# GLA stage of an encoder trunk on one Trainium2 core: query scaling moved to GpSimd, second key buffer moved, four output blocks accumulated together, and x loaded ahead of weight blocks 1 and 2

## The reference, cut to what matters

```
q, k, v, g, lr = split(h @ w_in)
gk = log_sigmoid(lr @ w_gk2 + b_gk) / 16          # one set per direction
q = q * GLA_HK ** -0.5
per direction, per chunk of 64 tokens:
    gcum = cumsum(gk)
    q_t = q * exp(gcum);  k_t = k * exp(-gcum)
    att = where(causal, q_t @ k_t^T, 0)
    o = att @ v + q_t @ state;  state = state * exp(g_end) + (k * exp(g_end - gcum))^T @ v
o = rmsnorm(forward + backward, norm_w) * silu(g)
return o @ w_out
```

## Time and profile before

| | us |
|---|---|
| Median of 3 runs (1442.85 to 1446.71) | 1443.49 |
| The profiled execution, its own time | 1441.75 |
| Its span, first to last instruction | 1439.6 |
| PE busy in the span | 1379.3 (96%) |
| DVE / ACT / POOL busy | 822.8 / 646.5 / 639.9 |

### The profile page before, as it was taken

How to read it: one execution, slowest core, us unless ns; L and a number is a source line. 1 busy time by engine, 2 the same in 40 slices (tenths; PEclk the granted TensorE clock), 3 DMA queues, 4 the chain that set the end, 5 groups by cost and what they waited for, 6 DMA issues and landing times.

```text
span 1439.6 us, 16672 instructions
## 1 busy us (share of the span) xinstructions
PE 1379.3 (96%) x6690; PEld 1138.9 (79%) x6690; DVE 822.8 (57%) x981; ACT 646.5 (45%) x985; POOL 639.9 (44%) x291
## 2 busy tenths in 40 slices
PE   6999988989999999999999999987999999999997
PEld 6778656767888888888888877875798888888886
DVE  5657597662027998887001654355168998884003
ACT  4544685554245544344323475434454544343221
POOL 2345495024533554545544243422714645445550
PEclk9999999999999999999999999998999999999998
DMA  5222100112322323323332312201213232323331
GB/s 188 86 92 88 37 1 19 33 45 88 99 77 90 101 93 98 95 95 94 93 95 86 114 59 88 88 30 44 73 45 131 89 102 89 102 85 94 96 92 59
DMA packets 36766, 117.89 MB, mean 82 GB/s; under 512 B 3857, under 2 KB 8337, under 8 KB 36689
## 3 DMA queue, kind: packets, MB, share of 16 engines
q1 hardware_dynamic: 35888, 114.63, 25.1%
q10 hardware_dynamic: 800, 2.20, 0.5%
HBM read 114.58 MB, written 2.10 MB: 81 GB/s over the span
## 4 chain that ended last, share of the span: by engine, by line
PE 76%; DVE 6%; ACT 3%; POOL 2%; issue 1%; DVEq 0%; ACTq 0%; POOLq 0%
PE bank L315 23%; PE bank L316 23%; PE bank L317 23%; PE bank L1169 1%; PE bank L1301 1%; POOL ebuf L987 1%; PE bank L1302 1%; POOL xdt L973 1%; PE bank L1777 1%; PE bank L1324 1%; DVE xres L562 1%; PE bank L405 1%; ACT prob L1373 1%; DVE m_ffn L555 0%; PE bank L1505 0%
## 5 line engine op out<-in xcount | busy, mean ns | idle before, releaser
L298 POOL TENSOR_TENSOR wlo<-raw,whi 128x1024 fp32r<-128x1024 f32 (+2 forms) x216 | 530.7, 2471 | 697.3 <-ACT whi L292 697.3
L315 PE MATMUL bank<-xw_hi,whi 128*128 128x512 f32 (+1 forms) x1360 | 516.6, 380 | 16.3 <-DVE xw_lo L581 11.7
L317 PE MATMUL bank<-xw_hi,wlo 128*128 128x512 f32 (+1 forms) x1360 | 505.8, 372 | 0.0
L316 PE MATMUL bank<-xw_lo,whi 128*128 128x512 f32 (+1 forms) x1360 | 505.8, 372 | 0.0
L292 ACT ACTIVATE whi<-raw 128x1024 fp32r<-128x1024 f32 (+2 forms) x217 | 220.6, 1023 | 216.5 <-DMA raw<-in_fout 111.8
L315 PEld LDWEIGHTS bank<-xw_hi,whi 128*128 128x128 f32 x1360 | 259.9, 191 | 67.8 <-issue 16.4
L316 PEld LDWEIGHTS bank<-xw_lo,whi 128*128 128x128 f32 x1360 | 259.8, 191 | 47.3 <-issue 3.6
L317 PEld LDWEIGHTS bank<-xw_hi,wlo 128*128 128x128 f32 x1360 | 259.5, 191 | 45.1
L534 DVE RECIPROCAL small<-small 128x2 f32<-128x2 f32 (+1 forms) x12 | 2.0, 170 | 352.7 <-ACT small L471 337.4
L638 DVE SCALAR_TENSOR_TENSOR cbuf<-ubuf,par,cbuf 128x510 f32<-128x510 f32 x100 | 170.8, 1708 | 3.5
L315 PE MATMUL bank<-g_hi,whi 128*128 128x512 f32 (+1 forms) x396 | 146.0, 369 | 0.1
(11 more groups left out here) (251 smaller groups left out, 1435.2 us busy)
## 6 DMA issues: line engine op xcount, KB each, us to landing
raw<-in_fin SPq DMA_DIRECT2D x88, 512.0 KB, 3.5
raw<-in_fout SPq DMA_DIRECT2D x32, 448.0 KB, 3.2
raw<-in_gin SPq DMA_DIRECT2D x25, 512.0 KB, 3.6
raw<-in_hin SPq DMA_DIRECT2D x24, 512.0 KB, 3.6
raw<-in_hout SPq DMA_DIRECT2D x16, 512.0 KB, 3.5
raw<-in_fout SPq DMA_DIRECT2D x16, 512.0 KB, 3.5
raw<-in_gout SPq DMA_DIRECT2D x8, 512.0 KB, 3.6
xres<-in_x SPq DMA_DIRECT2D x8, 256.0 KB, 7.5
```

What stands on the lines that cost most here:

```text
L298: engine.tensor_tensor(wlo[s][:, 0:n], raw[s][:, 0:n], whi[s][:, 0:n].bitcast(F32), ALU.subtract).then_inc(w_lo, 1)
L315: first = nc.tensor.matmul(out_ap, wh, ah, start=start, stop=False)
L316: nc.tensor.matmul(out_ap, wh, al, start=False, stop=False)
L317: return first, nc.tensor.matmul(out_ap, wl, ah, start=False, stop=stop)
```

## The change

1. **Queries on POOL.** DVE's two query operations leave `dve_keys`. A new `pool_queries` does them as plain products on POOL; the factor `QG` moves into the mask constants and into the scale of `cross_scores`.
2. **Second keys.** `kk1` now lies over the four `cbuf` buffers, which the stage's squares leave for new tiles `gsq`. So keys of n = 0 and 1 are both formed during the input projection, and queries 0 and 1 too, on POOL between two weight splits.
3. **Order.** Square roots (`deviation`) move behind the last exponentials on ACT and a one-column exponential stands at the head of ACT's stage; `spread(0)` to `spread(3)` move to the last head and beyond; `sums(2)` and `sums(3)` stay near their places. DVE does the gating after all keys, and takes over the low parts of chunks 2 to 7.
4. **Four output blocks together.** Output blocks 0 to 3 are accumulated in banks 0 to 3 head by head (`outs` in `pe_gla`): two chunks of the operand into four banks, as soon as that head is gated, with sums(3) and the last two spreads between. The high and low parts of weight blocks `gout` + 3, + 4, + 5 are made inside the stage; the following four stand before chunk 4 in `act_out` and `pool_out`.
5. **Start.** SP issues weight block 0, then the four x transfers of request 0, weight block 1, the four of request 1, weight block 2; ACT issues the parameters' DMA. ACT splits weight block 1 after all of request 0 and block 2 after all of request 1. PE takes block 0 for both requests piece by piece (48 matmuls of 256 columns), then blocks 1 and 2 with 24 matmuls of 512 columns each.

```diff
-            kk1 = sb("kk1", NREQ * NCH * SEQ, F32, s)      # over the operand's region
+            kk1 = sb("kk1", NREQ * NCH * SEQ, F32, s)      # over cbuf
+            gsq = [sb(f"gsq{i}", T, F32, s) for i in range(4)]
@@ pe_start
-                for j in range(GROUP[-1]):
-                    product(pe, j, of_request(banks[j], r), xw_hi, xw_lo, r=r, wait=r == 0, last_of_block=r == 1,
-                            by_chunk=("res_lo", r * KD) if j == 0 else None)
+                product(pe, 0, of_request(banks[0], r), xw_hi, xw_lo, r=r, wait=r == 0, last_of_block=r == 1,
+                        by_chunk=("res_lo", r * KD))
+            for j in (1, 2):
+                product(pe, j, banks[j][:], xw_hi, xw_lo)
@@ sync
-            sp.dma_start(par[:], params).then_inc(sem("par_in"), 16)
-                    if r == 0 and i % 2:
-                        load(sp, 1 + i // 2)
                     sp.dma_start(ckr(xres, 2 * i, r, 2), x_in[...])
+                load(sp, 1 + r)
@@ dve_gin, pool_gin
                     dve_keys(dve, 0)
+                    dve_zero_keys(dve, 1)
+                    dve_keys(dve, 1)
+                if at == BASE["gin"] + 21:
+                    pool_queries(pool, 0)
+                    pool_queries(pool, 1)
+        def pool_queries(pool, n):
...
+            pool.wait_ge(sem("gla_e"), 2 * n + 1)
+            nc.gpsimd.tensor_tensor(qt[d][:], ck(gqkv, hd), qt[d][:], ALU.mult).then_inc(sem("gla_q"), 1)
+            pool.wait_ge(sem("gla_q"), 2 * n + 1)
+            if hd:
+                pool.wait_ge(sem("gla_s"), n - 1)
+            nc.gpsimd.tensor_tensor(qx[d][...], qt[d][...][:, :, c0:c0 + 2],
+                                    carries_of(hd, d)[:, :, 6:8].unsqueeze(3).broadcast_to([P, NREQ, 2, CH]),
+                                    ALU.mult).then_inc(sem("gla_q"), 1)
@@ pe_gla
+            def outs(hd):
+                for c in range(GROUPED[2]):
+                    if hd == 0:
+                        pe.wait_ge(w_lo, base + c + 1)
+                    for k in (2 * hd, 2 * hd + 1):
+                        if c == 0:
+                            pe.wait_ge(sem("gla_lo"), k + 1)
+                        first, last = three(base + c, bank[c][:], ck(xw_hi, k), ck(xw_lo, k), k, k == 0, k == KD - 1)
+                    if hd == GLA_HEADS - 1:
+                        last.then_inc(mm, 1)
                 if hd < 3:
                     scores(2 * hd + 2)
+                if hd == 3:
+                    spread(0)
                 values(hd)
+                if hd == 3:
+                    spread(1)
                 if hd:
                     sums(hd - 1)
                 if hd < 3:
                     scores(2 * hd + 3)
-                if hd:
-                    spread(hd - 1)
-            sums(GLA_HEADS - 1)
-            spread(GLA_HEADS - 1)
+            outs(0)
+            sums(3)
+            spread(2)
+            outs(1)
+            spread(3)
+            outs(2)
+            outs(3)
@@ act_gla
+            nc.scalar.activation(small[:, 5:6], prm("eps"), ACT.Exp)
             act_gate_exps(act, 2)
             cross_scores(0, 0)
+            for hd in range(3):
+                act_gate_exps(act, 2 * hd + 3)
                 cross_scores(hd, 1)
+                if hd < 2:
+                    act_gate_exps(act, 2 * hd + 4)
                     cross_scores(hd + 1, 0)
+                    outs(hd)
+            cross_scores(3, 0)
+            deviation(0)
+            outs(2)
+            deviation(1)
+            cross_scores(3, 1)
+            act.wait_ge(sem("gla_s"), 8)
+            high(0)
+            hi(act, BASE["gout"] + 3)
+            outs(3)
+            deviation(2)
             high(1)
             deviation(3)
@@ dve_gla
+            for n in range(2, 8):
+                dve_keys(dve, n)
+                own_scores((n - 1) // 2, (n - 1) % 2)
+            diagonal(0)
+            own_scores(3, 1)
+            gated(0)
+            diagonal(1)
+            gated(1)
+            diagonal(2)
+            low(1)
+            gated(2)
             diagonal(3)
+            low(2)
             gated(3)
+            low(3)
@@ pool_gla
+            for n in range(2, 8):
+                pool_queries(pool, n)
+                if n in (4, 6):
+                    squares(n // 2 - 2)
+            squares(2)
...
+            lo(pool, nc.gpsimd, BASE["gout"] + 3)
             squares(3)
```

More of the change, by code:

```diff
@@ L127, in build_program @@
             prob1 = sb("prob1", 4 * SEQ, F32, s)
+        with ExitStack() as s:
+            kk1 = sb("kk1", NREQ * NCH * SEQ, F32, s)
         cbuf = [sb(f"cbuf{i}", T) for i in range(4)]
@@ L348, in x_norm, with obank @@
             return ((k + 1) // 2) * 32 + ((k + 1) % 2) * 16
-        def obank(c):
-            return bank[c % 2]
+        def obank(k, c):
+            return bank[c if c < GROUPED.get(k, 0) else c % 2]
         def late_bank(k, c, r):
@@ L365, in pe_out @@
             base = BASE[name]
-            for c in range(EARLY[k]):
-                if c >= 2:
+            for c in range(GROUPED.get(k, 0), EARLY[k]):
+                if k in GROUPED:
+                    pe.wait_ge(sem("out_m"), of("out_m", k) + c - GROUPED[k] + 1)
+                elif c >= 2:
                     pe.wait_ge(sem("out_m"), of("out_m", k) + c - 1)
@@ L375, in pe_out @@
                             pe.wait_ge(sem(stage), n)
-                    product(pe, base + c * per + b, obank(c)[:], src_hi, src_lo, k0=k0,
+                    product(pe, base + c * per + b, obank(k, c)[:], src_hi, src_lo, k0=k0,
                             start=b == 0, stop=b == per - 1, by_chunk=first_by_chunk if c == 0 and b == 0 else None)
@@ L447, in act_out @@
             for c in range(EARLY[k]):
-                for b in range(per):
-                    his(act, base + c * per + b)
+                if c >= GROUPED.get(k, 0):
+                    for at in range(base + (1 if k in GROUPED and c == GROUPED[k] else c * per), base + (c + 1) * per):
+                        his(act, at)
                 act.wait_ge(mm, base + (c + 1) * per)
@@ L452, in act_out @@
                     act.wait_ge(sem("out_acc"), of("out_acc", k) + c - 2)
[L453 removed]
+                nc.scalar.activation(sqacc[:] if c == 0 else cbuf[c % 2][:], obank(k, c)[:],
                                      ACT.Square).then_inc(sem("out_sq"), 1)
[L455 removed]
+                nc.scalar.activation(ck(m_tile, c), obank(k, c)[:], ACT.Copy,
                                      scale=prm("norm", m_norm(k) + c)).then_inc(sem("out_m"), 1)
@@ L521, in pool_out @@
             for c in range(EARLY[k]):
-                for b in range(per):
-                    los(pool, base + c * per + b)
+                if c >= GROUPED.get(k, 0):
+                    for at in range(base + (1 if k in GROUPED and c == GROUPED[k] else c * per), base + (c + 1) * per):
+                        los(pool, at)
                 if c:
@@ L1715, in dve_keys @@
                 nc.vector.tensor_tensor(to, k[:, :, c], e[:, :, c], ALU.mult).then_inc(sem("gla_kk"), 1)
-            nc.vector.scalar_tensor_tensor(out=qt[d][:], in0=ck(gqkv, hd), scalar=QG, in1=qt[d][:],
-                                           op0=ALU.mult, op1=ALU.mult).then_inc(sem("gla_q"), 1)
             dve.wait_ge(sem("gla_kk"), 5 * n + 2)
-            carries = carry[:].rearrange("p (m r j) -> p m r j", r=NREQ, j=8)[:, d * GLA_HEADS + hd]
+            carries = carries_of(hd, d)
             for c in range(NCH):
@@ L1823, in cross_scores @@
                                          sbank(d, r)[:, d * SEQ + (1 - d) * P:d * SEQ + (2 - d) * P],
-                                         ACT.Copy).then_inc(sem("gla_att_b" if d else "gla_att_f"), 1)
+                                         ACT.Copy, scale=QG).then_inc(sem("gla_att_b" if d else "gla_att_f"), 1)
             def outs(hd):
@@ L1915, in diagonal, with low @@
                                             sem("gla_diag"), 1)
-            dve_keys(dve, 1)
-            own_scores(0, 0)
-            dve_keys(dve, 2)
-            for hd in range(GLA_HEADS):
-                own_scores(hd, 1)
-                if hd < 3:
-                    dve_keys(dve, 2 * hd + 3)
-                if hd >= 2:
-                    gated(hd - 2)
-                if hd < 3:
-                    own_scores(hd + 1, 0)
-                    if hd < 2:
-                        dve_keys(dve, 2 * hd + 4)
-                if hd:
-                    diagonal(hd - 1)
+            def low(hd):
+                if hd == 1:
+                    dve.wait_ge(sem("gla_lo"), 2)
+                dve.wait_ge(sem("gla_o"), 2 * hd + 2)
+                for c in (2 * hd, 2 * hd + 1):
+                    dve.wait_ge(sem("gla_hi"), c + 1)
+                    nc.vector.tensor_tensor(ck(xw_lo, c), ck(gg, c), ck(xw_hi, c).bitcast(F32),
+                                            ALU.subtract).then_inc(sem("gla_lo"), 1)
+            own_scores(0, 0)
```

(17 more changed lines are left out.)

58 lines of the change are left out of this document (20 added, 38 removed).

## The result

The changed kernel takes **1432.69 us** in the median of five runs (1427.66 to 1433.35), the kernel before 1443.19 (five runs, 1442.76 to 1446.71): a ratio of 0.991 on record, 95% interval 0.989 to 0.993 (the two medians alone give 0.993). The five runs fall into two groups, 1427.66 and 1428.8, and 1432.69 to 1433.35. The profiled execution took 1432.82 us, with a span of 1431.0.

The account below looks back on a forecast made before the run. The prediction took PE, busy for 96% of the span, as the bound. Gains of 6.5 (start) and 17.0 (GLA stage), 23.5 us, took the profiled 1441.75 to 1418.3; with 1.7 for the median, rounded, 1420, range 1412 to 1430.

Parts of the forecast that it names:

- The step that failed: GLA stage, DVE products beside POOL: 0.7 us more per us of overlap, so keys 2 take 2.2 us.
- rival B: POOL holds DVE for a whole POOL instruction; GLA keys come later, 10 us less gain, 1430; chance 0.10.
- was to give 17.0: GLA stage: output block 3 ends at 1015.8 us, 17.0 before 1032.8.
- the clock's term of 1.5: GLA stage: 1.5 us allowed for PE time at the half clock, with 0 and 4 as ends.
- The wait at the third scores: GLA stage: PE waits for keys 2 from 952.2 us, so scores(2) starts at 954.1.
- the offload yields next to nothing: GLA keys: removed query work about 0.95 us of DVE, added contention about 0.8.
- was to give 6.5: Start: blocks 0 to 2 end at 27.5 instead of 34.4 us; 6.5 taken, bounds 3.3 and 8.0.
- The forecast's ends for DVE, 15.4 and 17.5: Start: DVE's last low part of x at 15.4 us, or 17.5 if one piece again takes 2.58 beside POOL's split.
- A: Start gives half: clock low to 22.4 us or x not earlier, 3.3 instead of 6.5, 1423; chance 0.13.
- C: The clock falls twice more or POOL's adds come late: 4 us less gain, 1424; chance 0.12.
- E: The gain doesn't arrive: a later stage waits for something that did not move, as a DMA; 1435; chance 0.05.
- D: Slower than before: POOL's query pairs become the GLA stage's chain, 1445 us and over; chance 0.03.

Follow-up runs that it names:

- queries_dve: The changed kernel with the queries of pairs 2 to 7 back on DVE, POOL keeping 0 and 1: 1423.6 us.
- queries_behind: The changed kernel with POOL's product of a later query waiting until DVE's five products of the same pair's keys are done: 1426.16 us.
- ungrouped: The changed kernel without the four output blocks opened together; all six run one after another from the end of the last spread: 1438.33 us.
- both_dve: The changed kernel with the queries of the six later pairs and the low parts of weight blocks 1 and 2 back on DVE: 1422.08 us.
- start_only: The kernel before with the change of the start alone: 1439.33 us, ratio 0.9978.
- pool_quarters: The changed kernel with POOL's low parts of weight blocks 1 and 2 made in four instructions of 256 columns each: 1424.05 us.
- scores0_early: both_dve with the first scores and the third pair's exponentials and keys moved ahead into the GLA input projection's last block: 1419.57 us.

## Why the prediction was wrong

**The step that failed: "So I give each product of DVE with two SBUF operands 0.7 us more for each us of overlap with POOL".** The contention isn't a share but a hold, rival B's mechanism. In these traces a DVE instruction with two tensor operands in SBUF that starts while a POOL instruction on SBUF operands runs ends only 0.1 to 0.6 us behind POOL's. So what it loses is the rest of POOL's instruction: a low part takes 2.39 and 2.59 us instead of 0.47 at the start, and the key products 1.83 and 2.19 against a forecast of 2.2 for all of them. I read the gating product's 1.40 against 0.69 as a rate; it started 0.4 us behind a POOL instruction of 1.27 us and was held by the rest of that. Nor does the 2.2 follow from the rate: 0.7 for each of 1.7 us of overlap, on 1.58 alone, is 2.8. In the changed kernel the same product takes 2.48 and 2.02 beside whole splits of POOL, while the scaling product before it (L1926), with one operand in PSUM, takes its usual 0.75 in the middle of such a split:

```profile
1005.71 2.39 POOL L302 TENSOR_TENSOR wlo<-raw,whi 128x1024 fp32r<-128x1024 f32 x1 [4.50 <-ACT whi L296]
1006.17 2.48 DVE L1930 TENSOR_TENSOR gg<-gg,ubuf 128x512 f32<-128x512 f32 x1
...
1011.72 2.60 POOL L302 TENSOR_TENSOR wlo<-raw,whi 128x1024 fp32r<-128x1024 f32 x1 [3.62 <-ACT whi L296]
1012.06 0.75 DVE L1926 SCALAR_TENSOR_TENSOR ubuf<-gqkv,par,bank 128x512 f32<-128x512 f32 x1
1012.85 2.02 DVE L1930 TENSOR_TENSOR gg<-gg,ubuf 128x512 f32<-128x512 f32 x1
```

The Trainium skill (SBUF — State Buffer, Who interferes with whom) calls the pair of ports that both engines share an exclusive lock. It says that a VectorE instruction with two SBUF inputs contends for it with a GpSimd instruction that reads SBUF, and that one with at most one SBUF input, outside the 2-port modes, does not. The traces agree: 2.48 and 2.02 for the first kind, 0.75 for the second. The prediction rested on the Trainium skill's GPSIMD Engine Reference (Key points), which names the contention without its form.

**The GLA stage** was to give 17.0 and gave 10.4 (112.3 to 101.9), and 14.7 once the queries no longer meet DVE's products (97.6). So the hold cost 4.3 us. PE's waits account for them: 3.6 + 4.1 + 0.2 = 7.9 us in the changed kernel, 2.1 + 0.9 + 0.5 = 3.5 in queries_dve. The clock does not: its mean from 943 to 1040 us is 0.95 in both. Rival B's price of 10 us was too high: PE has 8.7 us of work for each head's two pairs, and only the first pair's keys and the adds were exposed. The remaining 2.3 us I put to the clock's term of 1.5, with bounds of 0 and 4, which no run separates: at queries_dve's 10.2 us of half clock up to 5.1 us of PE's work is lost. Right were POOL's pair (1.27 to 1.38 and 0.62 to 0.88) and the end of the diagonals' waits (0.2 left). The wait at the third scores was to be 1.9 and is 2.1 in queries_dve, but there DVE makes the queries itself, so the match is luck; with the queries on POOL and no hold on the keys it is 3.4 (queries_behind). That the offload yields next to nothing was too kind: beside the keys it costs the 4.3. The four output blocks carry the stage's gain, as forecast: ungrouped is 9.7 us longer.

**The start** was to give 6.5 and gave 2.9. The forecast's ends for DVE, 15.4 and 17.5, allow for one part held by POOL; two were (2.39 and 2.59), as in the kernel before (2.36 and 2.58, of which the earlier trace rows show only the longer), and DVE ended at 18.5. From this PE's gap of 1.89 followed, and behind it 3.4 us at the half clock, for which the sum had no term. With the splits elsewhere the sums come at 28.02, as in the forecast (28), and the gain is 7.1. So the walk held but for the hold: the same cause as in the stage, on a row that I had in the earlier trace rows and priced only as a bound.

**What reached the end.** 2.9 + 10.4 = 13.3; the spans differ by 8.6. The stretch between sums and values is 3.6 us longer (907.3 to 910.9), and the rest 1.0. Of the 15 us between the forecast gain and that of the profiled execution, the stage has 6.6 (4.3 of them the hold), the start 3.6 (the hold), and these two 4.6, for which the sum had no term: the prediction assumed that whatever is gained in one place arrives. In the eleven profiles the stretch took 905.9 to 911.0. Two places in it can be named. One is a fall of the clock near 50 us. All eleven have the same wait of 2.9 us there, for a weight block's low part that POOL makes; behind it the changed kernel goes on at 1.2 GHz and queries_dve at 2.4. Below are the first matmul behind the wait in these two, and then the same stretch of before, of the changed kernel and of queries_dve:

```profile
47.32 0.76 PE L319 MATMUL bank<-xw_hi,whi 128*128 128x512 f32 x1 [2.94 <-POOL wlo L302]
```

```profile
47.54 0.47 PE L319 MATMUL bank<-xw_hi,whi 128*128 128x512 f32 x1 [2.94 <-POOL wlo L302]
```

```profile
40.00:60.00 20.00, 17.06 (x69) 13.55 (x68) 15.16 (x18) 11.55 (x16) 5.25 (x3) 0.91 0.25 75
```

```profile
40.00:60.00 20.00, 17.06 (x63) 13.51 (x62) 14.67 (x16) 11.24 (x15) 6.59 (x3) 0.83 0.24 77
```

```profile
40.00:60.00 20.00, 16.39 (x72) 12.99 (x71) 16.72 (x18) 12.92 (x17) 8.54 (x4) 1.00 0.26 80
```

The means of 0.91, 0.83 and 1.00 are 3.6, 6.8 and 0 us at half clock, of which about half is lost. The other place is PE's wait for POOL's products at L995 (L987 before): 2.1 us before and in queries_dve, 4.0 in the changed kernel and in both_dve. What decides which of them an execution gets, none of my runs shows. It need not be the change: the changed kernel and queries_dve have the same code up to the stage and differ here by 4.3 us, and the changed kernel's five runs span much the same 5 us. Nor do the runs say that the start's gain is always lost here. In start_only's profiled execution it was, in the medians of its twelve runs it was not. 0.9978 and 0.9919 multiply to 0.9897, within the interval of the whole.

**Rivals.** B was the mechanism and had 0.10. A's 3.3 us for the start are near the measured 2.9 by luck: its causes, a clock low to 22.4 or a late x, did not occur. C's clock fell once in the stage and stayed down for 10.2 us. E, a gain that doesn't arrive, had 0.05 and another cause, a transfer; 4.6 us were lost on the way. D (slower than before) did not come. That the hold takes from the start and from the stage at once was in no case of mine, and the range's upper end, B alone, was therefore too low.

## What to carry to other kernels

Before an elementwise instruction goes to POOL, look at which DVE instructions lie beside it: those with two tensors in SBUF wait for all that is left of POOL's instruction, those with one operand in PSUM do not. Offload beside the latter, or put POOL's work behind DVE's by a wait, which here took 4.5 us off the stage, or cut POOL's instruction in pieces so that DVE gets its turn. A wait of PE of 2 us can have a second price, the half clock behind it: give it a term with a bound of zero, since here the same wait of 2.9 us had it in some kernels and not in others. And a few us gained early should be given a loss on the way in the sum, where the same code in between varies by 5 us. A difference of that size between two kernels is then read from the stage that was changed, not from the whole time.

## What the runs showed of the hardware

The turns of pool_quarters: with POOL's instruction of 256 columns at 0.74 us when first, both engines' instructions take 0.91 to 0.95 us in the overlap, DVE's being 0.47 alone. In the overlap their starts alternate. So neither engine got a second turn while the other waited, and each also waited for the other's. The clock: a gap of 1.89 us at 16.2 was followed by 1.2 GHz from 19.5 on, and the gap of 3.62 us before 956.57 goes with 10 us at 0.56 on average. With gaps of at most 1.3 us in the stage (scores0_early) it stayed at 2.4 GHz. But the length of a gap doesn't settle it: behind the 2.9 us near 45 us it stayed at 2.4 GHz in queries_dve, queries_behind and ungrouped, and in queries_dve it fell to a mean of 0.57 from 981 to 985 us, with no gap over 0.94 us in the 30 us before.
